# The last two experts of a mixture-of-experts block: their products in another order, with buffers of their own

## The reference

```python
logits = (tok @ router_w) + router_b
topv, topi = lax.top_k(logits, 4)                      # 4 of 32 experts
combine = sum(one_hot(topi, 32) * softmax(topv)[..., None], axis=1)
for e in range(32):
    gu = tok @ w1[e] + b1[e]                           # 1024 -> 2048
    gate = minimum(gu[:, :1024], 7.0)
    lin = clip(gu[:, 1024:], -7.0, 7.0)
    act = (lin + 1) * gate * sigmoid(1.702 * gate)
    out = out + combine[:, e:e+1] * (act @ w2[e] + b2[e])  # 1024 -> 1024
return x + out
```

## Time and profile before

| | us |
|---|---|
| median of 3 runs | 1143.26 (1141.15 to 1143.31) |
| profiled execution | 1138.21 |
| its span, first to last instruction | 1136.5 |
| TensorE busy | 1084.6 (95%) |
| VectorE busy | 196.1 (17%) |
| ScalarE busy | 140.1 (12%) |
| chain that ended last | PE 64%, DMA 34% |

### The profile page before, as it was taken

How to read it: one execution, slowest core, us unless ns; L and a number is a source line. 1 busy time by engine, 2 the same in 40 slices (tenths; PEclk the granted TensorE clock), 3 DMA queues, 4 the chain that set the end, 5 groups by cost and what they waited for, 6 DMA issues and landing times.

```text
span 1136.5 us, 11852 instructions
## 1 busy us (share of the span) xinstructions
PE 1084.6 (95%) x4926; PEld 424.7 (37%) x4926; DVE 196.1 (17%) x503; ACT 140.1 (12%) x287; POOL 14.9 (1%) x34
## 2 busy tenths in 40 slices
PE   7999999999999999999999999999999999999997
PEld 5474544633333333333333333333333333333332
DVE  1630011312211111111111111111111111111101
ACT  2114111201100011010000000000000000000001
POOL 0004000000000000000000000000000000000000
PEclk9999999999999999999999999999999999999998
DMA  9824526799999999999999999999999999999995
GB/s 348 319 107 148 217 78 252 285 414 431 426 428 427 428 429 426 430 428 429 428 428 428 429 428 428 429 427 430 428 429 428 427 430 428 429 428 430 428 424 206
DMA packets 42069, 432.49 MB, mean 381 GB/s; under 512 B 4268, under 2 KB 5824, under 8 KB 17344
## 3 DMA queue, kind: packets, MB, share of 16 engines
q1 hardware_dynamic: 40416, 431.26, 90.6%
q10 hardware_dynamic: 1632, 0.95, 0.3%
HBM read 431.14 MB, written 1.05 MB: 380 GB/s over the span
## 4 chain that ended last, share of the span: by engine, by line
PE 64%; DMA 34%; DVE 0%; issue 0%; ACT 0%; SPq 0%; DVEq 0%; ACTq 0%
DMA ring<-in_expert_w_dram 34%; PE bank L330 23%; PE bank L345 12%; PE bank L1036 9%; PE bank L354 4%; PE bank L1192 2%; PE bank L1172 2%; PE bank L320 2%; PE bank L291 2%; PE bank L336 1%; PE bank L1097 1%; PE bank L307 1%; PE bank L312 1%; PE bank L1026 1%; PE bank L1119 0%
## 5 line engine op out<-in xcount | busy, mean ns | idle before, releaser
L330 PE MATMUL bank<-ring,work 128*64 128x512 f32 x2048 | 450.3, 594 | 16.3 <-DMA ring<-in_expert_w_dram 16.2
L330 PEld LDWEIGHTS bank<-ring,work 128*64 128x64 f32 x2048 | 142.7, 137 | 321.6 <-issue 280.5
L345 PE MATMUL bank<-ring,work 128*64 128x512 f32 x1024 | 230.7, 597 | 17.3 <-DMA ring<-in_expert_w_dram 16.8
L345 PEld LDWEIGHTS bank<-ring,work 128*64 128x64 f32 x1024 | 73.0, 137 | 168.6 <-issue 134.3
L925 DVE TENSOR_SCALAR work<-bank 128x512 f32<-128x512 f32 x31 | 21.4, 692 | 458.0 <-PE bank L330 458.0
L1036 PE MATMUL bank<-ring 128*128 128x512 f32 x224 | 98.5, 594 | 0.0
L698 ACT ACTIVATE work<-work 128x512 f32<-128x512 f32 x31 | 19.5, 630 | 495.7 <-DVE work L925 495.7
L354 PE MATMUL bank<-work,putT 64*128 64x512 f32 x256 | 63.6, 615 | 1.4 <-ACT work L714 1.4
L376 DVE TENSOR_TENSOR work<-bank,vecs 128x512 f32<-128x512 f32 x32 | 22.1, 692 | 227.8 <-PE bank L307 226.7
L1036 PEld LDWEIGHTS bank<-ring 128*128 128x128 f32 x224 | 41.8, 190 | 48.4 <-issue 48.2
L291 PE MATMUL bank<-xn,pick 128*64 128x512 f32 x248 | 58.5, 592 | 0.0
(11 more groups left out here) (185 smaller groups left out, 448.2 us busy)
## 6 DMA issues: line engine op xcount, KB each, us to landing
ring<-in_expert_w_dram SPq DMA_DIRECT2D x190, 2048.0 KB, 41.9
ring<-in_w_in_dram SPq DMA_DIRECT2D x8, 2048.0 KB, 19.2
ring<-in_w_out_dram SPq DMA_DIRECT2D x2, 2048.0 KB, 7.8
ring<-in_expert_w_dram SPq DMA_DIRECT2D x3, 1024.0 KB, 42.9
ring<-in_w_branch_attn_dram SPq DMA_DIRECT2D x1, 2048.0 KB, 8.4
ring<-in_w_branch_pool_dram SPq DMA_DIRECT2D x1, 2048.0 KB, 7.8
ring<-in_w_in_dram SPq DMA_DIRECT2D x1, 1296.0 KB, 7.5
xs<-in_x_dram SPq DMA_DIRECT2D x2, 512.0 KB, 4.0
```

The lines of the kernel that those rows point to most:

```text
L330: mm = pe.matmul(dst, hTe[:, at:at + SLOTS], w[:, col:col + BANK], start=(k == 0 and not bias_first), stop=(k == KD - 1 and bias_first), s ...
L345: mm = pe.matmul(ps_out[SLOTS * half:SLOTS * (half + 1), :], actT_e[:, at:at + SLOTS], w[:, col:col + BANK], start=(k == 0), stop=(k == KD ...
```

## The change

The end of the program is put into another order. The steady order of the loads is kept to the last expert (w1(31) ahead of w2(30)). TensorE computes up(31) ahead of down(30). Put transposes of expert 31 go to `ps_gather`, and the last expert has buffers of its own, laid over ones that are free by then: `putT_last` in `rows_e`, `actT_last` in `hTe`, `out_last` in `gate_e`, and its second product in `ps_gather`. The transposes of act(31) stand between the two chunks of down(30). The scatter of expert 30 is cut into its two tiles: tile 0 stands ahead of the last chunk, tile 1 behind it. The last chunk of w2(30) and the first of w2(31) come in two halves each, the last of w2(31) in three parts as before; the last chunk of w1(31) comes whole. The stores of the second 512 columns are issued by ScalarE.

```diff
+        putT_last, actT_last, out_last = rows_e[:, 0:TT * P], hTe, gate_e
-        TAIL = ((0, 2), (2, 3), (3, 4))
-        late_in = sem("late_in")
+        HALVES, THIRDS = ((0, 2), (2, 4)), ((0, 2), (2, 3), (3, 4))
+        TAIL = {(E - 2, 1): HALVES, (E - 1, 0): HALVES, (E - 1, 1): THIRDS}
         def w1_chunk(e, c):
-            if e == E - 1:
-                return CHUNKS - W1_CHUNKS - W2_CHUNKS + c
         def w2_chunk(e, c):
-            return at + c if e >= E - 2 else at + W1_CHUNKS + c
+            return at + c if e == E - 1 else at + W1_CHUNKS + c
...
+            def load_tail(e, c):
+                for i, (a, b) in enumerate(TAIL[e, c]):
+                    sp.dma_start(chunk_slot(w2_chunk(e, c))[:, a * D:b * D], w2_dram(e, c)[:, a * D:b * D]).then_inc(tail_in[e, c, i], 16)
             e = E - 2
-            sp.wait_ge(chunk_used, 4 * e - 2)
-            load_w2(e, 0)
-            sp.wait_ge(gemm1, e)
-            load_w2(e, 1)
-            sp.wait_ge(chunk_used, 4 * e - 1)
-            load_w1(e + 1, 0)
-            sp.wait_ge(gemm2, e - 1)
-            load_w1(e + 1, 1)
-            sp.wait_ge(chunk_used, 4 * e)
-            load_w1(e + 1, 2)
-            sp.wait_ge(chunk_used, 4 * e + 1)
...
+            sp.wait_ge(chunk_used, e * 4 - 2)
+            load_w1(e + 1, 0)
+            sp.wait_ge(gemm1, e)
+            load_w1(e + 1, 1)
+            sp.wait_ge(chunk_used, e * 4 - 1)
+            load_w1(e + 1, 2)
+            sp.wait_ge(gemm2, e - 1)
+            load_w1(e + 1, 3)
+            sp.wait_ge(chunk_used, e * 4)
+            load_w2(e, 0)
+            sp.wait_ge(chunk_used, e * 4 + 1)
+            load_tail(e, 1)
+            sp.wait_ge(chunk_used, e * 4 + 2)
+            load_tail(e + 1, 0)
             sp.wait_ge(gemm1, e + 1)
+            load_tail(e + 1, 1)
...
-            for j in range(2 * TT):
-                tt, cols = j // 2, slice((j % 2) * BANK, (j % 2 + 1) * BANK)
-                sp.wait_ge((s["result_dve"], s["result_act"])[j % 2], tt + 1)
-                sp.dma_start(out[0, tt * P:(tt + 1) * P, cols], xs[:, tt, cols]).then_inc(s["stored"], 16)
+            for tt in range(TT):
+                sp.wait_ge(s["result_dve"], tt + 1)
+                sp.dma_start(out[0, tt * P:(tt + 1) * P, 0:BANK], xs[:, tt, 0:BANK]).then_inc(s["stored"], 16)
...
-            out_out(E - 2)
-            putT_out(E - 1)
             for h in range(2):
                 act.wait_ge(gate_ok, E + h)
                 nc.scalar.activation(pairs(sig_e, h), pairs(gate_e, h), ACT.Sigmoid, scale=SWIGLU_ALPHA).then_inc(sig_ok, 1)
+            act.wait_ge(put_ps, E)
+            nc.scalar.copy(putT_last, ps_gather[:, 0:T]).then_inc(put_sb, 1)
             for h in range(2):
                 act.wait_ge(actT_ps, E + h)
-                nc.scalar.copy(actT_e[:, h * 2 * P:(h + 1) * 2 * P], (ps_gate, ps_lin)[h][:, h * 2 * P:(h + 1) * 2 * P]).then_inc(actT_sb, 1)
-            out_out(E - 1)
+                nc.scalar.copy(actT_last[:, h * 2 * P:(h + 1) * 2 * P], (ps_gate, ps_lin)[h][:, h * 2 * P:(h + 1) * 2 * P]).then_inc(actT_sb, 1)
+            out_out(E - 2)
+            act.wait_ge(gemm2, E)
+            nc.scalar.copy(out_last, ps_gather[:, :]).then_inc(out_ok, 1)
...
+            for tt in range(TT):
+                act.wait_ge(s["result_act"], tt + 1)
+                act.dma_start(out[0, tt * P:(tt + 1) * P, BANK:D], xs[:, tt, BANK:D]).then_inc(s["stored"], 16)
...
+            def down_tail(e, c, ps, actT):
+                for i, (a, b) in enumerate(TAIL[e, c]):
+                    pe.wait_ge(tail_in[e, c, i], 16)
+                    mm = down(pe, chunk_slot(w2_chunk(e, c)), c, range(a, b), ps, actT)
+                return mm
...
-            down_expert(0, E - 2)
-            pe.wait_ge(out_ok, E - 1)
-            scatter(pe)
-            transpose_put_expert(E - 1)
+            up_last()
+            pe.wait_ge(put_ok, E)
+            transpose_put(pe, ps_gather).then_inc(put_ps, 1)
             for j in range(2 * TT):
                 if j not in X1_FIRST:
                     add_x1(j)
-            up_last()
+            pe.wait_ge(actT_sb, E - 1)
+            pe.wait_ge(put_sb, E - 1)
+            pe.wait_ge(*chunk_landed(w2_chunk(E - 2, 0)))
+            down(pe, chunk_slot(w2_chunk(E - 2, 0)), 0)
             for h in range(2):
                 pe.wait_ge(glu_ok, E + h)
                 transpose_act(pe, range(2 * h, 2 * h + 2), (ps_gate, ps_lin)[h]).then_inc(actT_ps, 1)
-            down_last()
+            down_tail(E - 2, 1, ps_out, actT_e).then_inc(gemm2, 1)
+            pe.wait_ge(put_sb, E)
+            pe.wait_ge(actT_sb, E + 1)
+            down_tail(E - 1, 0, ps_gather, actT_last)
+            pe.wait_ge(out_ok, E - 1)
+            scatter(pe, None, range(0, 1))
+            down_tail(E - 1, 1, ps_gather, actT_last).then_inc(gemm2, 1)
+            scatter(pe, None, range(1, 2))
             pe.wait_ge(out_ok, E)
-            scatter(pe, acc_done)
+            scatter(pe, acc_done, range(TT), putT_last, out_last)
```

More of the change, by code:

```diff
@@ L176, in block_kernel @@
         chunk_in = [sem(f"chunk_in{i}") for i in range(RING)]
-        TAIL = ((0, 2), (2, 3), (3, 4))
-        tail_in = [sem(f"tail_in{i}") for i in range(len(TAIL))]
-        late_in = sem("late_in")
+        HALVES, THIRDS = ((0, 2), (2, 4)), ((0, 2), (2, 3), (3, 4))
+        TAIL = {(E - 2, 1): HALVES, (E - 1, 0): HALVES, (E - 1, 1): THIRDS}
+        tail_in = {(e, c, i): sem(f"tail_in{e}_{c}_{i}") for (e, c), parts in TAIL.items() for i in range(len(parts))}
         chunk_used = sem("chunk_used")
@@ L337, in transpose_act, with down @@
             return mm
-        def down(pe, w, c, rows=range(W2_ROWS)):
+        def down(pe, w, c, rows=range(W2_ROWS), ps=ps_out, actT=actT_e):
             for a in rows:
@@ L344, in down, with scatter @@
                     col = a * D + half * BANK
-                    mm = pe.matmul(ps_out[SLOTS * half:SLOTS * (half + 1), :], actT_e[:, at:at + SLOTS],
+                    mm = pe.matmul(ps[SLOTS * half:SLOTS * (half + 1), :], actT[:, at:at + SLOTS],
                                    w[:, col:col + BANK], start=(k == 0), stop=(k == KD - 1))
             return mm
-        def scatter(pe, done=None):
-            for tt in range(TT):
+        def scatter(pe, done=None, tiles=range(TT), at=putT, src=out_e):
+            for tt in tiles:
                 for half in range(2):
                     rows = halves(half)
-                    mm = pe.matmul(acc[2 * tt + half][:, :], putT[rows, tt * P:(tt + 1) * P], out_e[rows, :],
+                    mm = pe.matmul(acc[2 * tt + half][:, :], at[rows, tt * P:(tt + 1) * P], src[rows, :],
                                    start=False, stop=True, skip_group_check=True)
@@ L471, in _ @@
                     load_step(i, TURN + j)
+            def load_tail(e, c):
+                for i, (a, b) in enumerate(TAIL[e, c]):
+                    sp.dma_start(chunk_slot(w2_chunk(e, c))[:, a * D:b * D], w2_dram(e, c)[:, a * D:b * D]).then_inc(tail_in[e, c, i], 16)
             e = E - 2
-            sp.wait_ge(chunk_used, 4 * e - 2)
-            load_w2(e, 0)
-            sp.wait_ge(gemm1, e)
-            load_w2(e, 1)
-            sp.wait_ge(chunk_used, 4 * e - 1)
-            load_w1(e + 1, 0)
-            sp.wait_ge(gemm2, e - 1)
-            load_w1(e + 1, 1)
-            sp.wait_ge(chunk_used, 4 * e)
-            load_w1(e + 1, 2)
-            sp.wait_ge(chunk_used, 4 * e + 1)
[L485 to L489, removed]
+            sp.wait_ge(chunk_used, e * 4 - 2)
[7 more added lines that the diff above has]
+            sp.wait_ge(chunk_used, e * 4)
+            load_w2(e, 0)
+            sp.wait_ge(chunk_used, e * 4 + 1)
+            load_tail(e, 1)
+            sp.wait_ge(chunk_used, e * 4 + 2)
+            load_tail(e + 1, 0)
             sp.wait_ge(gemm1, e + 1)
-            n, src = w2_chunk(e + 1, 1), w2_dram(e + 1, 1)
-            for i, (a, b) in enumerate(TAIL):
-                sp.dma_start(chunk_slot(n)[:, a * D:b * D], src[:, a * D:b * D]).then_inc(tail_in[i], 16)
+            load_tail(e + 1, 1)
             sp.wait_ge(s["most_ok"], 1)
@@ L1314, in up_last @@
                 pe.wait_ge(hTe_ok, E)
-                for c in range(W1_CHUNKS - 1):
+                for c in range(W1_CHUNKS):
                     w, landed = chunk_at(0, w1_chunk(E - 1, c))
                     pe.wait_ge(*landed)
[L1318 to L1324, removed]
+                    mm = up(pe, w, c)
+                mm.then_inc(gemm1, 1)
             def down_expert(i, j):
```

## The result

The changed kernel takes 1134.42 us (median of 6 runs, 1132.38 to 1135.59) where the kernel before took 1141.32 us (6 runs, 1139.06 to 1143.31; three of them are those that the prediction had). The ratio is 0.9944, with a 95% interval from 0.9930 to 0.9959, or 6.4 us less. The profiled execution took 1134.28 with a span of 1132.5 (before 1138.21 and 1136.5).

What follows compares the result with a forecast made beforehand. The loop is bound by the expert weights, the end by TensorE's chain behind them. 5.1 us at the final scatter plus 0.4 for stores, 5.5 off 1143.26, gives 1137.8 us; range 1135.2 to 1140.6.

Steps and rivals of the forecast that it cites:

- the grid: Last weight loads: a 2048 KB chunk lands every 4.89 us, unchanged by the new order; the last part at 1121.2.
- TensorE's walk: From up(31) on: 1.0 us idle before w1(31)'s last chunk, final scatter at 1124.3 instead of 1129.36, 5.1 us earlier.
- Idle and clock at the gate: Gate of expert 31: idle of 2.31 and 0.29 us and 1.71 us for the slow clock would go.
- The cover of the gate: Gate of expert 31, 3.0 us, runs beside 5.6 us of TensorE work; uncovered, it would cost up to 3.0 us.
- The parts of the chunks: Finer loads of the last chunks: w2(31,1)'s parts are wanted 1.1 to 1.6 us after landing.
- The cut scatter: Expert 30's scatter: tile 1 behind the last product hides its 0.64 us copy and costs 0.3 us over it.
- Stores: Final stores: with ScalarE issuing two of the four, 0.4 us gained; bounds 0.7 gained to 0.6 lost.
- the starved stretch: Between SyncE's final stores: engines at 58 GB/s from 1132.75 to 1133.00; its length, 0.4 us, taken as the gain.
- The clock didn't fall: Rival at the last products, 10%: clock still falls from something other than the 2.31 us idle, costing 1.7 us; time 1139.5.
- The data-bound case: Rival at the last chunk, 12%: TensorE quicker than walked, the last part at 1121.2 sets the end; time 1136.7.
- ScalarE's stores landed: Rival at the final stores, 3%: those of ScalarE's queue land late, after up to 11.8 us; time 1146.5.
- The sum and its range: Whole kernel: 5.1 + 0.4 = 5.5 us off the median 1143.26, giving 1137.8; eight in ten from 1135.2 to 1140.6.

Runs made afterwards that it cites:

- e5: Changed kernel with one residual product ahead of the last chunk of w1(31); final scatter 41.87 us after TensorE's start on w2(29,1), ratio 0.9958 to the kernel before.
- e1: Kernel before with the two residual products moved behind up(31); 51.1 us from TensorE's start on w2(29,1) to the end, ratio 0.9970.
- e2: Changed kernel with the transposes of act(31) moved ahead of the residual; 53.0 us from TensorE's start on w2(29,1) to the end, 3.7 more.
- e3: Changed kernel with the last three chunks loaded whole; final scatter 43.67 us after TensorE's start on w2(29,1), 1.52 more than the changed kernel.
- e6: Changed kernel with both tiles of expert 30's scatter ahead of the last chunk; final scatter 42.79 us after TensorE's start on w2(29,1), 0.64 later.

## Why the prediction was wrong

The mechanism at the end of the kernel was right. What failed is the last step of the sum, the time that the gain was taken from, and the range around it; of the gain, the 0.4 us for the stores wasn't found.

*What bounds the kernel, the grid, the loads.* Right. Landings kept to 4.89 us, also in finer parts, as far as they are seen: the half that TensorE waited for in e5 landed 34.36 us after the counted start, where the prediction's walk had 1116.3 - 1082.0 = 34.3.

*TensorE's walk.* Right. It put the final scatter at 1124.3, 42.3 us after the counted start; it was 42.15. The largest miss inside it is the transposes of act(31), 0.68 us for 0.8. That up(31) began in the kernel before when two of its chunks had "long" been there holds for the first (by the grid at 1096.7); the second came 0.9 us ahead of the start.

*The terms of the gain.* Idle and clock at the gate: 3.4 us by e1, which took 1.9 of the 2.31 of idle and left the clock at 1.00 (1.71 in the prediction). The cover of the gate: 3.7 by e2. The parts of the chunks, which the prediction had in its walk and not as a term: 1.5 by e3. The cut scatter: 0.64 by e6. These don't add up to 5.2, as each is worth only what the others leave open.

*Stores.* Not confirmed. The prediction took 0.4 us for the starved stretch; from the final scatter on, both profiles have 7.14 us, and the twelve profiles give 0.1 with 0.4 either way. In the changed kernel's profile the stretch went, but landings grew. The rule from the Trainium skill (DMA: Bandwidth & Descriptors, Issuing engines are not separate DMA queues), that a second issuer saves only the time of initiating, bounded it rightly, at nothing to the starved stretch; the measured 0.1 lies between, and these profiles don't tell the two ends apart. ScalarE also issued earlier than the prediction had it: its first store goes at 1127.32, ahead of the end of its second copy, not behind it.

*The rivals.* The clock didn't fall (1.00 through the last products), and e1 and e2 tie the fall at the gate to the idle: with 1.94 us it fell, with 0.40 and 0.29 it did not. The Trainium skill (TensorE: Matmul & The Clock Gate, Why this matters for your kernels) speaks of gaps above some 3 us; the measurement decides, and here less than 2 was enough. The data-bound case was nearer than its 1.1 us of room said, as e5 showed, but it lay at another part than the prediction named. Its own walk had that part: the second half of w2(31,0) at 1116.3, wanted at 1117.0, is 0.7 us of room, and 1.1 holds for the last chunk alone. ScalarE's stores landed after 3.2 us, not 11.8.

*The sum and its range.* This is the step that failed. 5.5 us came off 1143.26, the median of three runs, with the reasoning that the level didn't matter. It did: the same kernel had 1141.32 with three more runs, and medians of 1139.3 to 1139.9 later. The level alone makes 1.9 us of the miss of 3.4, the rest is 6.9 between the medians for 5.5, which the end of the kernel doesn't explain: it gave 5.2. The three runs that the prediction started from, 1141.15 to 1143.31, lie where every later run of this kernel had a mean clock of 0.994 or 0.995. So they were most likely executions with one more fall of the clock far ahead of the changed code; their own clocks aren't on record. The profiled execution of the kernel before stood there with 1138.21, 5 us under the median, and its mean clock of 0.997 held nothing but the fall at the gate and one behind the last matmul; I noted the distance and didn't ask what it was made of. A group of executions 5 us faster than the median of three means that the next median can move by some us both ways. With 1138.21 as the low end, 1138.2 - 5.5 = 1132.7, the range would have held the time. That is said with the result known.

## What to carry to other kernels

A gate that TensorE must wait for costs twice where the idle lowers the clock (here 1.9 us of idle and 1.7 of slow products); look for work without dependence on it, already in the program, that can change its place, before making buffers for more. When the last chunks are within a microsecond of being wanted, walk every part against its landing, not only the last. When the median and the profiled execution of the same kernel are five microseconds apart, find out what parts them before taking either as the level.

## What the runs showed of the hardware

The clock of TensorE fell to 0.50 behind an idle of 1.94 or 2.31 us at the gate, and stood at 1.00 through idles of 1.0 us in the loop. Near 220 us it fell behind idles of at most 0.57 us in some executions and not in others of one program, which no run here explains.

Stores of 256 KB by one queue landed after 2.0 to 3.0 us, by two queues at once after 2.5 to 4.1. Four of them, all ready at once, took 4.09 us by one queue and 4.12 by two.

With the same program the first projection took 7.14 us or 8.6 to 9.4, at a granted clock that the rows give as 1.00 in both.
